# The state-space group norm of three groups, moved to later slots of the weight stream

## The chip, the cores and the metric

The kernel runs on one core of a Trainium2 chip. Its time is the device time of one execution in microseconds (us); a run gives the median of several. TensorE multiplies matrices, VectorE, ScalarE and GpSimd work on vectors, and SyncE issues DMAs. Each engine takes its instructions in order and waits on semaphores that others raise.

## What is computed

The reference is a network of four layers, two of one kind (`first_block`) and two of another (`second_block`), on 256 tokens of width 1024. The change touches only the state-space branch of the first kind, which occurs twice:

```
proj = einsum('bld,de->ble', rms_norm(h, norm1_w[l]), w_in[l])
z, xbc, dt_f, dt_b, sc_b, sc_c, sc_v = split(proj)
y_f, y_b = ssd_chunked(...), flip(ssd_chunked(flip(...)))     # 16 heads of 64, 4 groups of 4 heads, two directions
y = y_f + y_b + xs * d_skip
y = y.reshape(bsz, length, 1024) * silu(z)                      # the gate
yg = y.reshape(bsz, length, 4, 256)                             # four groups of 256 channels
yg = yg * rsqrt(mean(yg * yg, axis=-1) + RMS_EPS)               # the group norm
y_ssd = yg.reshape(bsz, length, 1024) * norm_w
h = h + einsum('ble,ed->bld', concatenate([y_ssd, y_sc]), w_out[l])
```

The other half of the mix, `y_sc`, is a short convolution of three further parts of `proj`.

## The kernel before

All weights are read once. They come in chunks of 128 x 2048 values (1 MB). A chunk is loaded by SyncE into one of three raw buffers. It is then split into a high part (fp32r, `split_hi`, ScalarE, L1231) and a low part (raw minus high, `split_lo`, VectorE, L1671), each in two halves of 128 x 1024, into one of two buffers. TensorE multiplies high weights by high and low inputs, and low weights by high inputs, 48 weight loads and matmuls for a chunk (L542). A split into a buffer waits until the chunk before last is multiplied (`chunk_done`), so ScalarE and VectorE split chunk c + 2 while TensorE multiplies chunk c + 1.

Around this stream the order of everything else is written out by hand, in slots. Slot c is what an engine does between chunk c and the next: on TensorE after the matmuls of chunk c (`slot(c)`), on ScalarE and VectorE around their split of chunk c + 2. There, `late(c)` stands before the split and `extras(c)` behind it. In a layer of the first kind chunks 0 to 8 are xbc and dt, 9 to 12 are z, 13 to 24 are the short convolution's three parts in turn, and 25 to 32 are w_out (25 to 28 for `y_sc`, 29 to 32 for `y_ssd`).

The 16 heads are worked on in pairs p = 0 to 7. In slot 10 + 2p ScalarE makes the first head's decays (`drops(p, 0)`: four operations, L1317), their exp (L1322), and the second head's four (`drops(p, 1)`). Their exp is in `late` of slot 11 + 2p. In that slot VectorE multiplies both by the masked scores (`heads_decayed`, L1863). In slot 12 + 2p TensorE multiplies by the inputs (`heads(p)`, L872). SyncE loads the decay rows for the next pair (L419) once the pair's exps are done.

A group g is two pairs, and its norm goes through six steps:

- `group_gate(g)`, VectorE: adds the skip to the heads' sums (two operations, L1879), multiplies by the gate (L1881).
- `group_squares(g)`, ScalarE: L1326.
- `group_norm(g)`, TensorE: sums of squares by matmuls with ones (L880).
- `group_rsqrt(g)`, VectorE: sums times 1/256 plus eps (`ask_roots`, L1699), a power by GpSimd (L1137), and two diagonal matrices (`root_diagonals`, L1706).
- `group_spread(g)`, TensorE: ones times diagonals, which gives the roots in all partitions (L888).
- `group_scale(g)`, VectorE (L1891), `group_hi(g)`, ScalarE (L1330), and `group_lo(g)`, VectorE (L1898): the scaled output and its two parts, the inputs of w_out.

`GROUP_END` is {14: 0, 18: 1, 22: 2, 26: 3}. Gate and squares of a group are in the slot of its second pair, sums and roots one slot later, spread and the rest two slots later. `group_hi` stands in front of `drops` in ScalarE's extras, and `group_squares` behind them. The gate of a group waits until the low part of the group before is made, since both use the buffer `yb`. Odd groups use another PSUM bank than even ones. VectorE's short-convolution work lies in the same slots: in 14, 17, 20 and 23 a product (L1971) ahead of `late`, and the outer taps (L1846, L1849) behind the split; in 15, 18, 21 and 24 a product (L1981) ahead of `late`, and a low part (L1987) behind the split. ScalarE begins slots 13, 16, 19 and 22 with a copy (L1390) that VectorE waits for.

Of the kernel before, what the change touches and what calls it, by code (L numbers as in the profile page):

```python
# [11 lines left out]
TOK = SEQ // P  # L12
# [4 lines left out]
GROUPS = 4  # L17
# [169 lines left out]
DT_CHUNK = 1  # L187
PAIR_SLOTS = [12, 14, 16, 18, 20, 22, 24, 26]

GROUP_END = {PAIR_SLOTS[2 * g + 1]: g for g in range(GROUPS)}  # L190
ROW_SLOTS = [c - 2 for c in PAIR_SLOTS]
EARLY_TAPS = 3
CONV_OPS = {2: 4, 3: 2, 4: 7, 5: 4, 6: 4, 7: 4, 8: 4, 9: 9, 10: 8, 11: 4, 12: 4, 13: 4, 14: 2, 15: 2, 16: 2, 17: 2, 18: 4, 19: 8, 20: 8,
# [6 lines left out]
def build(nc, a, consts, out):  # L200
# [4 lines left out]
    with ExitStack() as ctx:  # L205
# [66 lines left out]
        sums = sqb[0:32, 2:4, :]  # L272
# [11 lines left out]
        acc = [ctx.enter_context(nc.psum_tensor(f"bank{i}", [P, 512], f32)) for i in range(4)]  # L284
# [39 lines left out]
        y2_ready, gsq_ready, gstat, gdiag, gbc = sem("y2_ready"), sem("gsq_ready"), sem("gstat"), sem("gdiag"), sem("gbc")  # L324
        y3_ready, y_hi, mixssd_ready = sem("y3_ready"), sem("y_hi"), sem("mixssd_ready")
# [199 lines left out]
        def _(pe):  # L525
# [290 lines left out]
            for l in range(DEPTH):  # L816
# [58 lines left out]
                def group_norm(g):  # L875
                    b = acc[2 + g % 2]
                    pe.wait_ge(gsq_ready, l * 4 + g + 1)
                    for m in range(2):
                        for t in range(TOK):
                            last = mm(b[:, t:t + 1], sqb[:, m, t * P:(t + 1) * P], K("ones", 1),  # L880
                                      start=m == 0 and t == 0, stop=m == 1, skip_group_check=True)
                    last.then_inc(gstat, 1)

                def group_spread(g):
                    b = acc[2 + g % 2]
                    pe.wait_ge(gdiag, l * 4 + g + 1)
                    for t in range(TOK):
                        last = mm(b[:, t * P:(t + 1) * P], K("ones"), diag[:, t, :], start=True, stop=True)  # L888
                    last.then_inc(gbc, 1)

                def slot(c):

                    if c in PAIR_SLOTS:
                        heads(PAIR_SLOTS.index(c))
                    if c - 1 in GROUP_END:
                        group_norm(GROUP_END[c - 1])
                    if c - 2 in GROUP_END:
                        group_spread(GROUP_END[c - 2])

                for c in range(1, 25):  # L900
                    if c == DT_CHUNK:
# [4 lines left out]
                    if c == 5:  # L906
                        pe.wait_ge(dta_ready, l + 1)
                        pe.sem_inc(waited, 1)
                        for i in range(2):
                            for t in range(TOK):  # L910
                                k = 2 * i + t
# [37 lines left out]
                for j in range((FF_PAIRS - 1) // 2):  # L949
                    for i in range(2):  # L950
                        c, x = C1_FFN + 2 + 3 * i, cx + j * 6
# [16 lines left out]
            for l in range(DEPTH):  # L968
# [114 lines left out]
                for q in range(2):  # L1083
                    for i in range(2):
                        for t in range(TOK):
                            k = 2 * q + i
# [19 lines left out]
                for j in range((FF2_PAIRS - 1) // 3):  # L1106
                    for i in range(3):
                        c, x = C2_FF + 1 + 2 * i, cx + j * 6
# [3 lines left out]
                        n = l * FF2_PAIRS + j * 3 + (DEPTH * FF_PAIRS + i + 1)  # L1112
# [105 lines left out]
        def _(act):  # L1218
# [64 lines left out]
            for l in range(DEPTH):  # L1283
# [5 lines left out]
                if l == 0:  # L1289
                    act.wait_ge(pt_ready, 2)  # L1290
                    for q in range(DEPTH):
                        for i in range(2):
                            off, n = P1_LATE + 88 * i, 88 + 2 * i
# [30 lines left out]
                def group_squares(g):  # L1324
                    act.wait_ge(y2_ready, l * 4 + g + 1)
                    A(sqb[:, 0:2, :], yb, ACT.Square).then_inc(gsq_ready, 1)  # L1326

                def group_hi(g):
                    act.wait_ge(y3_ready, l * 4 + g + 1)
                    A(hidh[:, 2 * g:2 * g + 2, :], yb, ACT.Copy).then_inc(y_hi, 1)  # L1330
# [5 lines left out]
                def extras(c):  # L1336
                    if c == 5:
                        act.wait_ge(dtT, l + 1)
                        A(dtok[:].rearrange("p a b -> p (a b)"), acc[0][:, 0:128], ACT.Copy).then_inc(dtok_ready, 1)
                    if c == 6:  # L1340
                        act.wait_ge(cs_done, l + 1)
                        A(sums, acc[2][0:32, :].rearrange("p (d t) -> p d t", d=2), ACT.Copy).then_inc(sums_ready, 1)
                        A(diag[:, 2, :], acc[3][:, 0:128], ACT.Copy).then_inc(cs_ready, 1)
                    if c - 2 in GROUP_END:
                        group_hi(GROUP_END[c - 2])
                    if c in ROW_SLOTS:
                        p = ROW_SLOTS.index(c)
                        drops(p, 0)
                        heads_exp(p, 0)
                        drops(p, 1)  # L1350
                    if c in GROUP_END:
                        group_squares(GROUP_END[c])

                for c in range(9):
                    multiplied(c, cx)
# [9 lines left out]
                    for m in range(2):  # L1365
                        k = 2 * q + m
# [8 lines left out]
                for q in range(4):  # L1375
                    c = 9 + q
# [10 lines left out]
                for j in range(4):  # L1387
                    c, u = 13 + 3 * j, 12 + 3 * j
# [8 lines left out]
                    for m in range(2):  # L1397
                        k = 2 * j + m
# [68 lines left out]
                for j in range((FF_PAIRS - 1) // 2):  # L1467
                    for i in range(2):
                        x, xr, y = cx + j * 6, cr + j * 2, ux + j * 4
                        c = C1_FFN + 2 + 3 * i  # L1470
# [25 lines left out]
            for l in range(DEPTH):  # L1496
# [69 lines left out]
                for c in range(28):  # L1566
# [16 lines left out]
                    else:  # L1583
                        k = 2 * (c - 16)
# [16 lines left out]
                for q in range(2):  # L1601
                    act.wait_ge(conv_back, l * 2 + q + 1)
                    for m in range(2):
                        k = 2 * q + m
# [36 lines left out]
                for j in range((FF2_PAIRS - 1) // 3):  # L1641
                    for i in range(3):
                        x, xr, y = cx + j * 6, cr + j * 2, ux + j * 3
                        c = C2_FF + 1 + 2 * i
# [14 lines left out]
        def _(dve):  # L1659
# [37 lines left out]
            def ask_roots(sums, n, scale):  # L1697

                ts(small[:, 16:16 + n], sums, scale, EPS, MUL, ADD).then_inc(spread_var, 1)  # L1699

            def root_diagonals(k, n, signal):

                y = small[:, 24:24 + n]
                dve.wait_ge(spread_root, k + 1)
                for i in range(n):
                    last = ts(diag[:, i, :], ident, y[:, i:i + 1], None, MUL)  # L1706
                last.then_inc(signal, 1)

            def rsqrt_diagonals(k, sums, n, scale, signal):

                ask_roots(sums, n, scale)
                root_diagonals(k, n, signal)

            def root(r, t, centred):

                v, y = norm_small[:, 2, t:t + 1], norm_small[:, 3, t:t + 1]
# [120 lines left out]
            for l in range(DEPTH):  # L1837
# [34 lines left out]
                def group_gate(g):  # L1872

                    if g == 0:
                        dve.wait_ge(pc_ready, l * 2 + 2)
                    dve.wait_ge(y_done, l * 8 + 2 * g + 2)
                    for m in range(2):
                        k = 2 * g + m
                        chain(stt(out=yb[:, m, :], in0=xbc[:, k, :], scalar=p1("d_skip", k), in1=half(acc[2 + g % 2], m), op0=MUL, op1=ADD))  # L1879
                    chain.sync()  # L1880
                    stt(out=yb, in0=yb, scalar=0.5, in1=zz[:, 2 * g:2 * g + 2, :], op0=MUL, op1=MUL).then_inc(y2_ready, 1)  # L1881

                def group_rsqrt(g):
                    dve.wait_ge(gstat, l * 4 + g + 1)
                    rsqrt_diagonals(l * 4 + g, acc[2 + g % 2][:, 0:TOK], TOK, 1.0 / 256, gdiag)

                def group_scale(g):
                    dve.wait_ge(gbc, l * 4 + g + 1)
                    for m in range(2):
                        k = 2 * g + m  # L1890
                        last = stt(out=yb[:, m, :], in0=yb[:, m, :], scalar=p1("ssd_norm", k), in1=acc[2 + g % 2][:, 0:SEQ], op0=MUL, op1=MUL)  # L1891
                        if m == 0:
                            chain(last)
                    last.then_inc(y3_ready, 1)

                def group_lo(g):
                    dve.wait_ge(y_hi, l * 4 + g + 1)
                    tt(hidl[:, 2 * g:2 * g + 2, :], yb, hidh[:, 2 * g:2 * g + 2, :].bitcast(f32), SUB).then_inc(mixssd_ready, 1)  # L1898
# [6 lines left out]
                def extras(c):  # L1905
                    if c in (7, 8):
                        t = c - 7
                        for q in range(2):
                            dve.wait_ge(xT_done, l * 4 + 2 * t + q + 1)
                            b = acc[2 * t + q][:, :].rearrange("p (h d) -> p h d", d=64)  # L1910
                            for d in range(2):
                                col = dtok[:, t, 16 * d + 8 * q:16 * d + 8 * q + 8].unsqueeze(2).to_broadcast([P, 8, 64])
                                tt(xdt[:, d, t, 512 * q:512 * q + 512].rearrange("p (h d) -> p h d", d=64), b, col, MUL).then_inc(xdt_ready, 1)
                    if c in (9, 10):
                        for g in range(2 * (c - 9), 2 * (c - 8)):
                            mask_scores(g)
                    if c - 2 in GROUP_END:
                        group_scale(GROUP_END[c - 2])
                    if c - 2 in GROUP_END:
                        group_lo(GROUP_END[c - 2])  # L1920
                    if c in GROUP_END:
                        if GROUP_END[c]:
                            dve.wait_ge(mixssd_ready, l * 4 + GROUP_END[c])
                        group_gate(GROUP_END[c])
                    if c - 1 in GROUP_END:
                        group_rsqrt(GROUP_END[c - 1])

                for c in range(9):
                    multiplied(c, cx)
# [24 lines left out]
                for q in range(4):  # L1954
                    c = 9 + q
# [7 lines left out]
                for j in range(4):  # L1963
                    c, u = 13 + 3 * j, 12 + 3 * j
# [93 lines left out]
                for j in range((FF_PAIRS - 1) // 2):  # L2058
                    for i in range(2):
                        x, y = cx + j * 6, ux + j * 4  # L2060
                        c = C1_FFN + 2 + 3 * i
# [20 lines left out]
            for l in range(DEPTH):  # L2082
# [114 lines left out]
                for c in range(28):  # L2197
                    kind, b = list2[c][0], ring[c % RING]
                    if kind == "gate":
                        k = 2 * (c - 16)  # L2200
# [256 lines left out]
```

## Time and profile before

| | |
|---|---|
| median of 3 runs | 1683.14 us (1682.93 to 1683.48) |
| the profiled execution | 1682.33 us, span 1680.5 us |
| mean granted TensorE clock | 0.998 |
| busy: TensorE matmul, weight load | 1662.5 us (99%), 1481.4 us (88%) |
| busy: VectorE, ScalarE, GpSimd | 1331.1 us (79%), 980.9 us (58%), 64.4 us (4%) |
| landing of a decay-row load, median | 4.7 us from its issue |

The profile is of one execution. Busy shares are over the whole span. Matmuls are pipelined and their ends are modelled, so TensorE is read best from its weight loads (PEld), whose starts and idle times are recorded. In a timeline a row is a group of like instructions in order of time. The slots 12 to 32 of the first layer lie between about 94 and 226 us, those of the second between about 499 and 631.

### The profile page before, as it was taken

The numbers are of one execution on the slowest core, as the hardware profiler recorded it, in microseconds if no ns is written. First come the engines' busy times: TensorE is split into PE (matmuls) and PEld (weight loads), VectorE is DVE, ScalarE is ACT, GpSimd is POOL, SyncE is SP. The second block draws the span as 40 slices with busy tenths as digits, with TensorE's granted clock in tenths as the row PEclk, the third lists the DMA queues.
The fourth block names the chain that finished last, engine by engine and source line by source line (L and its number), as shares of the span: only waits on it lengthen the run. The fifth ranks groups of instructions, "written<-read, shape, count | busy, mean of one in ns | idle before, by whom it ended". The sixth has DMA issues, their size and how long they took to land.

```text
span 1680.5 us, 27054 instructions
## 1 busy us (share of the span) xinstructions
PE 1662.5 (99%) x10683; PEld 1481.4 (88%) x10690; DVE 1331.1 (79%) x2077; ACT 980.9 (58%) x1631; POOL 64.4 (4%) x79
## 2 busy tenths in 40 slices
PE   9999999999999999999999999999999999999998
PEld 7999888888999988888899889888879988978886
DVE  7877678888877758888899998766679999786666
ACT  5567556565757656666644875545454487555444
POOL 2000000000200000000000011000000000100000
PEclk9999999999999999999999999999999999999999
DMA  7665555555556646555466454656547645466553
GB/s 241 187 190 176 180 172 195 183 199 163 176 176 190 189 161 203 190 197 190 162 203 200 151 188 154 212 188 196 180 148 225 203 150 176 156 208 200 187 190 100
DMA packets 237788, 308.11 MB, mean 183 GB/s; under 512 B 6531, under 2 KB 198749, under 8 KB 237661
## 3 DMA queue, kind: packets, MB, share of 16 engines
q1 hardware_dynamic: 237353, 306.26, 56.7%
q8 instruction: 85, 1.39, 0.4%
q14 instruction: 42, 0.34, 0.1%
q10 hardware_dynamic: 308, 0.12, 0.0%
HBM read 301.04 MB, written 1.11 MB: 180 GB/s over the span
## 4 chain that ended last, share of the span: by engine, by line
PE 88%; DVE 8%; ACT 2%; issue 1%; POOL 0%; POOLq 0%; DVEq 0%; ACTq 0%
PE ring_banks L542 65%; PE bank L542 17%; DVE weights_lo L1671 3%; DVE conv_sums L2110 1%; PE bank L872 1%; PE bank L981 1%; PE bank L992 1%; PE ring_banks L784 1%; ACT weights_hi L1231 1%; PE bank L880 0%; PE bank L832 0%; PE bank L1017 0%; ACT decay L1317 0%; PE bank L797 0%; DVE pair L2241 0%
## 5 line engine op out<-in xcount | busy, mean ns | idle before, releaser
L1671 DVE TENSOR_TENSOR weights_lo<-raw_weights,weights_hi 128x1024 fp32r<-128x1024 f32 (+1 forms) x550 | 643.5, 1211 | 98.4 <-ACT weights_hi L1231 97.2
L542 PE MATMUL ring_banks<-input_parts,weights_hi 128*128 128x256 f32 (+1 forms) x4000 | 691.6, 325 | 5.3 <-DVE weights_lo L1671 2.0
L1231 ACT ACTIVATE weights_hi<-raw_weights 128x1024 fp32r<-128x1024 f32 (+1 forms) x552 | 544.2, 1036 | 194.3 <-PE bank L542 94.9
L542 PEld LDWEIGHTS ring_banks<-input_parts,weights_hi 128*128 128x128 f32 x4000 | 592.8, 190 | 67.8 <-issue 9.9
L542 PE MATMUL ring_banks<-input_parts,weights_lo 128*128 128x256 f32 x2752 | 373.7, 283 | 0.0
L542 PEld LDWEIGHTS ring_banks<-input_parts,weights_lo 128*128 128x128 f32 x2752 | 356.7, 191 | 7.3
L542 PE MATMUL bank<-weights_hi,hidden_hi 128*128 128x512 f32 x432 | 111.3, 392 | 0.0
L542 PE MATMUL bank<-weights_hi,hidden_lo 128*128 128x512 f32 x432 | 110.0, 389 | 0.0
L542 PE MATMUL bank<-weights_lo,hidden_hi 128*128 128x512 f32 x432 | 109.9, 389 | 0.0
L2110 DVE SCALAR_TENSOR_TENSOR conv_sums<-conv_padded,params_second_layer,conv_sums 128x256 f32<-128x256 f32 x240 | 99.2, 480 | 0.0
L542 PEld LDWEIGHTS bank<-weights_hi,hidden_lo 128*128 128x128 f32 x432 | 81.1, 188 | 16.9
L542 PEld LDWEIGHTS bank<-weights_lo,hidden_hi 128*128 128x128 f32 x432 | 81.1, 188 | 16.9
L542 PEld LDWEIGHTS bank<-weights_hi,hidden_hi 128*128 128x128 f32 x432 | 78.0, 189 | 14.1
L1633 ACT ACTIVATE pair<-ring_banks,params_second_layer 128x256 f32<-128x256 f32 x64 | 26.9, 472 | 101.3 <-PE ring_banks L542 101.2
L2339 DVE TENSOR_TENSOR pair<-ring_banks,pair 128x512 f32<-128x512 f32 x32 | 22.1, 691 | 71.9 <-ACT pair L1633 71.9
L542 PE MATMUL ring_banks<-weights_hi,hidden_hi 128*128 128x512 f32 x192 | 75.7, 394 | 0.0
L542 PE MATMUL ring_banks<-weights_hi,hidden_lo 128*128 128x512 f32 x192 | 74.8, 390 | 0.0
L2018 DVE TENSOR_TENSOR pair<-ring_banks,pair 128x512 f32<-128x512 f32 x42 | 29.0, 692 | 40.0 <-ACT pair L1443 31.1
L542 PE MATMUL ring_banks<-weights_lo,hidden_hi 128*128 128x512 f32 x192 | 49.4, 392 | 0.0
L1317 ACT ACTIVATE decay<-squares,diagonals 128x256 f32<-128x256 f32 (+1 forms) x128 | 47.4, 442 | 0.3 <-DMA squares<-decay_rows 0.3
L1863 DVE TENSOR_TENSOR decay<-decay,masked_scores 128x768 f32<-128x768 f32 x32 | 29.7, 955 | 22.2 <-ACT pair L1390 11.4
L542 PE MATMUL ring_banks<-hidden_hi,weights_hi 128*128 128x256 f32 x192 | 47.1, 285 | 0.0
(267 smaller groups left out, 1703.8 us busy)
## 6 DMA issues: line engine op xcount, KB each, us to landing
raw_weights<-in_w_in SPq DMA_DIRECT2D x103, 1024.0 KB, 5.3
raw_weights<-in_w_ff SPq DMA_DIRECT2D x64, 1024.0 KB, 5.5
raw_weights<-in_w_ffn_up SPq DMA_DIRECT2D x44, 1024.0 KB, 5.1
raw_weights<-in_w_ffn_down SPq DMA_DIRECT2D x22, 1024.0 KB, 4.9
raw_weights<-in_w_out SPq DMA_DIRECT2D x16, 1024.0 KB, 5.2
squares<-decay_rows SPq DMA_DIRECT2D x16, 512.0 KB, 4.7
raw_weights<-in_w_o SPq DMA_DIRECT2D x8, 1024.0 KB, 5.1
pair<-pair SPq DMA_DIRECT2D x64, 64.0 KB, 2.9
```

Of the source, the lines that this page charges most:

```text
L542: return mm(o, w, x, start=first, stop=last, skip_group_check=True)
L784: mm(b[:, :], zt[:, 0:P], zt[:, :], start=True, stop=True, skip_group_check=True)
L872: last = mm(o, xdt[:, d, t, h * 64:h * 64 + 64], decay[:, i, e0:e0 + n], start=e0 == 0, stop=e0 == 384)
L981: last = mm(acc[r][:, lo:hi], q, k, start=True, stop=True)
L1231: A(whi[:, t, i * n:(i + 1) * n], raw[:, s, i * n:(i + 1) * n], ACT.Copy).then_inc(hi_done, 1)
L1317: chain(A(decay[:, i, e0:e0 + n], head_rows[:, r0 // SEQ, i, r0 % SEQ:r0 % SEQ + n], ACT.Relu, bias=cs_tok[:, k, e:e + 1], scale=-1.0))
L1633: last = A(tmp[gs % 3][:, m, :], wide_low(u + gx)[:, m, :], ACT.Identity, bias=pc2[:, ds(k, 1)], scale=1.0)
L1671: tt(wlo[:, t, r], raw[:, s, r], whi[:, t, r].bitcast(f32), SUB).then_inc(w_ready, 1)
L1863: tt(decay[:, i, :], decay[:, i, :], scores[:, h // 4, :], MUL).then_inc(v_ready, 1)
L2018: tt(b[:], wide_high(u + side), b[:], ADD).then_inc(ring_free, 1)
L2110: ins = stt(out=cacc[:, k, :], in0=src, scalar=w, in1=cacc[:, k, :], op0=MUL, op1=ADD)
L2339: tt(t[:], wide_high(u + gx), t[:], ADD).then_inc(ring_free, 1)
```

## The change

Four tables, one for each kind of step, take the place of `GROUP_END`. For groups 0 to 2 the gate and the squares move one slot later, the sums and the root's request one later, the diagonals two later (and away from the request), and the spread, the scale, hi and lo two later. Sums and spreads now stand in slots in which TensorE has heads, behind them. For group 3 nothing moves, but scale, hi and lo of group 2 now stand ahead of its gate in slot 26. No instruction is added or removed.

```diff
@@ -187,7 +187,10 @@
 DT_CHUNK = 1
 PAIR_SLOTS = [12, 14, 16, 18, 20, 22, 24, 26]
 
-GROUP_END = {PAIR_SLOTS[2 * g + 1]: g for g in range(GROUPS)}
+GATE_SLOTS = {15: 0, 19: 1, 23: 2, 26: 3}
+SUM_SLOTS = {16: 0, 20: 1, 24: 2, 27: 3}
+DIAGONAL_SLOTS = {17: 0, 21: 1, 25: 2, 27: 3}
+SPREAD_SLOTS = {18: 0, 22: 1, 26: 2, 28: 3}
 ROW_SLOTS = [c - 2 for c in PAIR_SLOTS]
 EARLY_TAPS = 3
 CONV_OPS = {2: 4, 3: 2, 4: 7, 5: 4, 6: 4, 7: 4, 8: 4, 9: 9, 10: 8, 11: 4, 12: 4, 13: 4, 14: 2, 15: 2, 16: 2, 17: 2, 18: 4, 19: 8, 20: 8,
@@ -892,10 +895,10 @@
 
                     if c in PAIR_SLOTS:
                         heads(PAIR_SLOTS.index(c))
-                    if c - 1 in GROUP_END:
-                        group_norm(GROUP_END[c - 1])
-                    if c - 2 in GROUP_END:
-                        group_spread(GROUP_END[c - 2])
+                    if c in SUM_SLOTS:
+                        group_norm(SUM_SLOTS[c])
+                    if c in SPREAD_SLOTS:
+                        group_spread(SPREAD_SLOTS[c])
 
                 for c in range(1, 25):
                     if c == DT_CHUNK:
@@ -1341,15 +1344,15 @@
                         act.wait_ge(cs_done, l + 1)
                         A(sums, acc[2][0:32, :].rearrange("p (d t) -> p d t", d=2), ACT.Copy).then_inc(sums_ready, 1)
                         A(diag[:, 2, :], acc[3][:, 0:128], ACT.Copy).then_inc(cs_ready, 1)
-                    if c - 2 in GROUP_END:
-                        group_hi(GROUP_END[c - 2])
+                    if c in SPREAD_SLOTS:
+                        group_hi(SPREAD_SLOTS[c])
                     if c in ROW_SLOTS:
                         p = ROW_SLOTS.index(c)
                         drops(p, 0)
                         heads_exp(p, 0)
                         drops(p, 1)
-                    if c in GROUP_END:
-                        group_squares(GROUP_END[c])
+                    if c in GATE_SLOTS:
+                        group_squares(GATE_SLOTS[c])
 
                 for c in range(9):
                     multiplied(c, cx)
@@ -1706,11 +1709,6 @@
                     last = ts(diag[:, i, :], ident, y[:, i:i + 1], None, MUL)
                 last.then_inc(signal, 1)
 
-            def rsqrt_diagonals(k, sums, n, scale, signal):
-
-                ask_roots(sums, n, scale)
-                root_diagonals(k, n, signal)
-
             def root(r, t, centred):
 
                 v, y = norm_small[:, 2, t:t + 1], norm_small[:, 3, t:t + 1]
@@ -1880,9 +1878,9 @@
                     chain.sync()
                     stt(out=yb, in0=yb, scalar=0.5, in1=zz[:, 2 * g:2 * g + 2, :], op0=MUL, op1=MUL).then_inc(y2_ready, 1)
 
-                def group_rsqrt(g):
+                def group_root(g):
                     dve.wait_ge(gstat, l * 4 + g + 1)
-                    rsqrt_diagonals(l * 4 + g, acc[2 + g % 2][:, 0:TOK], TOK, 1.0 / 256, gdiag)
+                    ask_roots(acc[2 + g % 2][:, 0:TOK], TOK, 1.0 / 256)
 
                 def group_scale(g):
                     dve.wait_ge(gbc, l * 4 + g + 1)
@@ -1914,16 +1912,17 @@
                     if c in (9, 10):
                         for g in range(2 * (c - 9), 2 * (c - 8)):
                             mask_scores(g)
-                    if c - 2 in GROUP_END:
-                        group_scale(GROUP_END[c - 2])
-                    if c - 2 in GROUP_END:
-                        group_lo(GROUP_END[c - 2])
-                    if c in GROUP_END:
-                        if GROUP_END[c]:
-                            dve.wait_ge(mixssd_ready, l * 4 + GROUP_END[c])
-                        group_gate(GROUP_END[c])
-                    if c - 1 in GROUP_END:
-                        group_rsqrt(GROUP_END[c - 1])
+                    if c in SPREAD_SLOTS:
+                        group_scale(SPREAD_SLOTS[c])
+                        group_lo(SPREAD_SLOTS[c])
+                    if c in GATE_SLOTS:
+                        if GATE_SLOTS[c]:
+                            dve.wait_ge(mixssd_ready, l * 4 + GATE_SLOTS[c])
+                        group_gate(GATE_SLOTS[c])
+                    if c in SUM_SLOTS:
+                        group_root(SUM_SLOTS[c])
+                    if c in DIAGONAL_SLOTS:
+                        root_diagonals(l * 4 + DIAGONAL_SLOTS[c], TOK, gdiag)
 
                 for c in range(9):
                     multiplied(c, cx)
```

## Rows read from the trace of the kernel before

**Rows 1.** The page: the chain of work that ended last, by engine.

```profile
PE 88%; DVE 8%; ACT 2%; issue 1%; POOL 0%; POOLq 0%; DVEq 0%; ACTq 0%
```

**Rows 2.** Waits of TensorE's weight loads: us in total, times, longest us.

```profile
PEld bank L880 <- ACT squares L1326: 1.2, 4, 0.3
```

**Rows 3.** Busy time in one stretch, granted clock, DMA share, GB/s.

```profile
225.00:236.00 11.00, 10.79 (x76) 8.99 (x76) 7.84 (x20) 6.88 (x15) 1.11 (x2) 1.00 0.29 96
```

**Rows 4.** Timeline of TensorE's weight loads, layer 0: start, us, line, [idle before].

```profile
109.24 3.90 PEld L542 LDWEIGHTS ring_banks<-input_parts,weights_hi 128*128 128x128 f32 x32 [0.17 <-issue]
...
143.36 0.97 PEld L880 LDWEIGHTS bank<-constants,squares 128*128 128x128 f32 x8 [0.32 <-ACT squares L1326]
...
165.24 3.90 PEld L542 LDWEIGHTS ring_banks<-input_parts,weights_hi 128*128 128x128 f32 x32 [0.17 <-issue]
...
170.98 0.98 PEld L880 LDWEIGHTS bank<-constants,squares 128*128 128x128 f32 x8
171.89 3.90 PEld L542 LDWEIGHTS ring_banks<-input_parts,weights_hi 128*128 128x128 f32 x32
...
177.84 1.28 PEld L872 LDWEIGHTS bank<-decay,x_times_dt 128*64 128x64 f32 x16
179.29 0.52 PEld L888 LDWEIGHTS bank<-diagonals,constants 128*128 128x128 f32 x4 [0.17 <-DVE diagonals L1706]
179.73 0.19 PEld L542 LDWEIGHTS ring_banks<-weights_hi,hidden_hi 128*128 128x128 f32 x1
...
192.30 0.19 PEld L542 LDWEIGHTS ring_banks<-weights_hi,hidden_hi 128*128 128x128 f32 x1 [0.17 <-issue]
...
197.65 1.08 PEld L880 LDWEIGHTS bank<-constants,squares 128*128 128x128 f32 x8
```

**Rows 5.** Timeline of VectorE in the same stretch.

```profile
115.30 0.69 DVE L1981 TENSOR_TENSOR pair<-pair,ring_banks 128x512 f32<-128x512 f32 x1 [0.67 <-PE ring_banks L542]
116.20 1.83 DVE L1863 TENSOR_TENSOR decay<-decay,masked_scores 128x768 f32<-128x768 f32 x2 [0.21 <-ACT decay L1322]
117.94 2.35 DVE L1671 TENSOR_TENSOR weights_lo<-raw_weights,weights_hi 128x1024 fp32r<-128x1024 f32 x2
120.21 0.69 DVE L1987 TENSOR_TENSOR hidden_lo<-pair,hidden_hi 128x512 fp32r<-128x512 f32 x1
120.81 0.16 DVE L1699 TENSOR_SCALAR small<-bank 128x2 f32<-128x2 f32 x1
...
126.13 0.87 DVE L1891 SCALAR_TENSOR_TENSOR diagonals<-diagonals,params_first_layer,bank 128x256 f32<-128x256 f32 x2
...
141.05 0.87 DVE L1879 SCALAR_TENSOR_TENSOR diagonals<-xbc,params_first_layer,bank 128x256 f32<-128x256 f32 x2
...
144.09 1.83 DVE L1863 TENSOR_TENSOR decay<-decay,masked_scores 128x768 f32<-128x768 f32 x2 [1.44 <-ACT pair L1390]
...
175.91 0.88 DVE L1846 SCALAR_TENSOR_TENSOR pair<-pair,params_first_layer 128x255 f32<-128x255 f32 x2
...
177.62 0.15 DVE L1699 TENSOR_SCALAR small<-bank 128x2 f32<-128x2 f32 x1
178.59 0.48 DVE L1706 TENSOR_SCALAR diagonals<-constants,small 128x128 f32<-128x128 f32 x2 [0.81 <-POOL small L1137]
```

**Rows 6.** Timeline of ScalarE in the same stretch.

```profile
127.03 0.63 ACT L1330 ACTIVATE hidden_hi<-diagonals 128x512 fp32r<-128x512 f32 x1 [2.26 <-DVE diagonals L1891]
127.57 1.48 ACT L1317 ACTIVATE decay<-squares,diagonals 128x256 f32<-128x256 f32 x4
129.08 0.84 ACT L1322 ACTIVATE decay<-decay 128x768 f32<-128x768 f32 x1
129.83 1.48 ACT L1317 ACTIVATE decay<-squares,diagonals 128x256 f32<-128x256 f32 x4
...
143.28 0.60 ACT L1390 ACTIVATE pair<-ring_banks 128x512 f32<-128x512 f32 x1
...
144.51 2.00 ACT L1231 ACTIVATE weights_hi<-raw_weights 128x1024 fp32r<-128x1024 f32 x2
```

## The prediction

> **What bounds the kernel now.** I read the page first. The chain that ended last is 88% TensorE and 8% VectorE [rows 1]: weight chunks follow one another on TensorE without a pause. Next came the waits of the weight-load side of TensorE, where a stall shows most cleanly. In the whole span its waits for the squares of the group norm (L880) come to 1.2 us over 4 waits [rows 2]. So all that the present placing of the norm costs TensorE is those 1.2 us. The granted clock is 1.00 in a stretch where TensorE was idle several tenths [rows 3]. Then I read the three engines' timelines of layer 0, slots 15 to 28; layer 1 repeats them. Each layer has two of the four waits, in slots 15 and 19, of 0.3 us each.
>
> **What TensorE's own order costs.** From weight load to weight load [rows 4]: a w_in chunk takes 5.74 us to a norm (165.24 to 170.98), 5.95 to heads (171.89 to 177.84); heads take 1.45 (177.84 to 179.29, with 0.17 idle), a norm's sums 0.91, a spread 0.44. The chunk before the last norm, of w_out, takes 5.35. The change has three fewer stops per layer between chunks, but the stop itself costs nothing that goes away: chunk to norm has no idle, and the 0.21 and 0.17 around heads stay. Sums behind heads stand nowhere in the trace; heads to spread and heads to chunk are the nearest, and say 0.17 at most either way. I take 0, and keep 6 x 0.17 = 1.0 us both ways for the range. So TensorE's work is unchanged, and all turns on when the squares are ready.
>
> **The chain that ends at the sums.** From the start of the gate on VectorE to the start of the sums is 2.31 us, two passes, one product, the squares on ScalarE (141.05 to 143.36) [rows 4, 5]. I now follow the new order, slot by slot. Before, the gate follows the outer taps in an even slot, which has no decays. The new slots 15, 19 and 23 are the odd ones, where VectorE also does both decay products (116.20 to 117.94, 1.74), and TensorE's only grace is that heads (1.45) come first in the next slot.
>
> *Group 0, gate in slot 15.* Chunk 15 is done at 115.30 as now. VectorE: 0.90 to the decays, 1.74 decays, 2.27 weight split, 0.60 low product [rows 5], gate at 120.8, sums possible at 123.1. TensorE: without the sums in slot 15 chunk 16 starts at 109.24 + 5.74 = 114.98, heads at 120.93, sums' turn at 122.38. Wait 0.7 us; now it is 0.3.
>
> *Group 1, gate in slot 19.* TensorE goes on at 123.1 + 0.91 = 124.0 (chunk 17), 129.8 (18), 135.7 heads, 137.2 spread of group 0, 137.6 (19). Chunk 18 is done at 129.8 + 6.06 = 135.8, where 6.06 is start to release (109.24 to 115.30). VectorE in slots 17 and 18: product when chunk 17 is done (130.1), 0.60, decays 1.74, split 2.27, taps 1.71 (175.91 to 177.62), diagonals 0.48 (178.59), giving 136.4 to 136.9: the diagonals stand 0.2 us before the spread wants them. Then product 0.90, split 2.27, low product 0.60: the scale starts at 140.5. ScalarE has had the hi split done since about 137.8 and sits in front of the hi part of group 0 until scale + 0.90 = 141.4 (126.13 to 127.03 [rows 5, 6]); behind it in its queue stand the decays of pair 4. These take 0.54 + 1.51 + 0.75 + 1.51 = 4.3 us (127.03, 127.57, 129.08, 129.83 [rows 6]). So the copy that opens slot 19 starts at 145.8, though chunk 19 was done at 137.6 + 6.06 = 143.6: ScalarE is 2.1 us late. VectorE waits for that copy: decays at +0.81 (143.28 to 144.09), 146.6; split 148.3; gate 150.6; sums possible at 152.9. TensorE: chunk 20 at 143.3, heads at 149.3, sums' turn at 150.7. Wait 2.1 to 2.2 us; now 0.32. Today the same ScalarE stall falls in slot 16 and is made good by slot 18, whose gate has no decays ahead of it.
>
> *Group 2, gate in slot 23.* Let chunk 23 start at t. VectorE: done t + 6.06, product 0.60, decays 1.74, and 0.6 more because the second exp is late. (In slot 22 ScalarE reaches the hi part of group 1 at t + 2.9 and ends the decays' second exp 0.54 + 1.51 + 0.75 + 1.51 + 0.84 later, at t + 8.1; VectorE would want it at t + 7.5.) Then 0.1 to the split, 2.27 split, 1.71 taps, 2.31: t + 15.4. TensorE: 5.74 + 5.95 + 1.45 = t + 13.1. Wait 2.2 us, of which 1.6 stand even if ScalarE were on time. Now it is 0.
>
> *Group 3, gate still in slot 26*, but scale and low part of group 2 now stand ahead of it. From chunk 26 done: hi split's first half 1.1 (half of the 2.00 of the two at 144.51, and the start), lo split 2.27, scale to hi part 0.90 and hi part to low part 0.67 (126.13, 127.03, 127.70), low part 0.60, gate chain 2.31: 7.8. TensorE: heads 1.45, spread 0.44, chunk 27 5.35, less 0.1: 7.1. Wait 0.7 us; now none (197.65 follows 192.30 by the work alone [rows 4]).
>
> **What goes and gives nothing.** The square-root trip over GpSimd no longer stands between ask and diagonals for three groups, about 0.8 us of VectorE idleness each. After the ask in slots 16 and 20 VectorE has to wait for the next chunk anyway, so this hides. ScalarE's squares leave slots 14, 18 and 22, where the decays of the next pair are made, but the two chains above start from waits, and not from that work. The decay-row loads on SP's queue follow the second exp of each pair, and land about 5 us later (the page's median is 4.7), which is before they are wanted: the exp of slot 19 ends at 147.1, the decays for which the rows are loaded start at 155.5. No DMA and no instruction is added. Heads of group 2 need the scale of group 0 (new: 140.5, wanted 149.3): still ahead. The w_out chunks 31 and 32 need group 3's low part, in slot 28 as before: 5.5 us ahead, as now.
>
> **The sum.** Per layer 0.7 + 2.15 + 2.2 + 0.7 = 5.75 us of waits, less 0.6 to 0.7 of today's: +5.1; two layers +10.2. The same walk over the old order gives waits of 0.3, 0.4, 0.1 and 0 where the rows have 0.3, 0.3, 0, 0, so it errs high by about 0.1 a wait; I take +10. Nothing gives it back: TensorE is the chain before and after the stretch, and the splits run one or two chunks ahead. The profiled execution took 1682.33 us (span 1680.5), 0.8 below the median 1683.14 of the runs. 1682.33 + 10 = 1692.3 profiled, and 1693.0 as a median.
>
> **A rule of the skill.** The rows show clock 1.00 through TensorE waits of a few tenths [rows 3]; none has a wait of 2 us in mid-kernel. The Trainium skill, "TensorE: Matmul & The Clock Gate" (HAM oscillation — how this bites in real kernels), says that too long an idle gap makes the gate fall back to half rate, so that the next burst starts cold. Whether the new waits are long enough for that no row here can tell; it is the third rival.
>
> **Rivals.**
> 1. *The waits vanish (not slower).* Heads in front of the sums give 1.45 us of cover, the spread gets a slot of its own, and no stall is left: two layers lose 2 x 0.6. 1683.1 - 1.2 = 1681.9. For it speaks that ScalarE and VectorE are at 58% and 79%. Against it: the chain of slot 23 holds 1.6 us without any lateness elsewhere. It decides at one point: whether the gate of slots 19 and 23 starts within 2.31 us of the end of the heads, or before. Chance 4%, with "the change moves nothing that TensorE feels".
> 2. *Half of it.* ScalarE isn't late in slot 19, because the scale of slot 18 comes earlier than I have it; then group 1 waits 0.1, and group 2 1.6: 0.7 + 0.1 + 1.6 + 0.7 - 0.6 = 2.5 per layer, 1688.1. For it: all depends on one queue order. Against: the rows of slot 16 now show the same 2.26 us stall of ScalarE in front of a hi part and the same 4.3 us behind it. Chance 8%.
> 3. *The clock falls in the 2 us waits.* The four long ones would each be followed by matmuls at 1.2 GHz. One chunk after each at half rate costs at most its own 5.74 again, so up to 4 x 5.7 on top: 1700 to 1716. Chance 3%.
> 4. *The lateness feeds itself.* ScalarE and VectorE, now waiting for each other across slots, let a weight split come late as well, and TensorE waits for weights too. The split of chunk 21 ends at 150.6 against a chunk start at 153.8: 3 us of room. If that were gone in one slot per layer, 1695 to 1699. Chance 5%.
>
> **How the numbers follow.** The forecast has 80%, its own range 1690.5 to 1695.0 (eight waits at 0.2 each, 1.0 for the sums behind heads, 0.3 of the runs). For the range I go 1 us further towards rival 2: 1689.5 to 1695.0. A change of 0.2%, 3.4 us, is about what can be told from none. Slower by more: the forecast, rivals 3 and 4, nearly all of rival 2: 0.93. Within: rival 1 and some of 2: 0.05. Faster by more has no mechanism: 0.02.
>
> **What would show it.** After: the weight-load side waits for the squares at L880 eight times, about 11 us in all, near 0.7, 2.1, 2.2, 0.7 in each layer, in slots 16, 20, 24 and 27, and the chunks themselves keep their spacing. ScalarE's longest waits for the scale stand in slot 18. VectorE's waits for GpSimd's roots fall from eight to two. TensorE's clock stays at 1.00. If the L880 waits in slots 20 and 24 are below 1 us, the order of ScalarE's queue was read wrongly; if they are as said and the time doesn't follow, TensorE had room that the page doesn't show.

## The result, and the profile after

The changed kernel takes 1698.93 us (median of 4 runs, 1697.42 to 1699.89) against 1683.18 us before (1682.93 to 1683.48). The ratio is 1.0092, with a 95% interval of 1.0079 to 1.0105: slower by 15.75 us. Forecast were 1693.0 and at most 1695.0. The direction and the place are as forecast, and 6 us more are lost than the sum had. The profiled execution took 1698.79 us, its span is 1697.0 us, the mean granted clock 0.994 (before 0.998).

The page after, its chain of work by engine (as [rows 1]) and by line:

```profile
PE 85%; DVE 10%; ACT 2%; issue 2%; DMA 0%; POOL 0%; SPq 0%; DVEq 0%; POOLq 0%; ACTq 0%
PE ring_banks L545 63%; PE bank L545 17%; DVE weights_lo L1674 4%; DVE conv_sums L2109 1%; PE bank L984 1%; ACT decay L1320 1%; PE bank L995 1%; DVE decay L1861 1%; ACT weights_hi L1234 1%; PE bank L883 0%; PE bank L835 0%; DVE diagonals L1877 0%; PE bank L1020 0%; PE bank L875 0%; DVE diagonals L1879 0%
```

TensorE has gone from 88% to 85% of the chain and VectorE from 8% to 10%: more of the time now passes while TensorE waits. The waits of its weight loads for the squares (as [rows 2]; lines after L190 have moved by three, so L880 is L883):

```profile
PEld bank L883 <- ACT squares L1329: 12.7, 8, 2.4
```

Eight waits and 12.7 us, where there were four and 1.2 us. Their places, in the timeline of TensorE's weight loads in layer 0 (as [rows 4]; start, us, line, idle before):

```profile
121.06 1.28 PEld L875 LDWEIGHTS bank<-decay,x_times_dt 128*64 128x64 f32 x16
123.24 0.97 PEld L883 LDWEIGHTS bank<-constants,squares 128*128 128x128 f32 x8 [0.90 <-ACT squares L1329]
...
149.44 1.28 PEld L875 LDWEIGHTS bank<-decay,x_times_dt 128*64 128x64 f32 x16
152.82 0.97 PEld L883 LDWEIGHTS bank<-constants,squares 128*128 128x128 f32 x8 [2.10 <-ACT squares L1329]
153.71 5.40 PEld L545 LDWEIGHTS ring_banks<-input_parts,weights_hi 128*128 128x128 f32 x32
159.04 1.99 PEld L545 LDWEIGHTS ring_banks<-input_parts,weights_lo 128*128 128x128 f32 x16
...
180.53 1.28 PEld L875 LDWEIGHTS bank<-decay,x_times_dt 128*64 128x64 f32 x16
184.23 0.97 PEld L883 LDWEIGHTS bank<-constants,squares 128*128 128x128 f32 x8 [2.43 <-ACT squares L1329]
185.12 0.19 PEld L545 LDWEIGHTS ring_banks<-weights_hi,hidden_hi 128*128 128x128 f32 x1
...
199.75 0.19 PEld L545 LDWEIGHTS ring_banks<-weights_hi,hidden_hi 128*128 128x128 f32 x1
...
206.00 0.97 PEld L883 LDWEIGHTS bank<-constants,squares 128*128 128x128 f32 x8 [0.91 <-ACT squares L1329]
```

The four L883 rows are slots 16, 20, 24 and 27. From heads to sums 1.45 us are work, so the waits proper are 123.24 - 121.06 - 1.45 = 0.73, 152.82 - 149.44 - 1.45 = 1.93, 184.23 - 180.53 - 1.45 = 2.25, and 206.00 - 199.75 - 5.35 = 0.90 us. The forecast had 0.7, 2.15, 2.2 and 0.7. In layer 1 the two long ones are the same to 0.01 us. The new thing is behind the second one: the 32 high weight loads of chunk 21 take 153.71 to 159.04, 5.33 us, where those of chunk 23 take 3.82 in the kernel before. The granted clock, in windows of 1 us each (as in [rows 3]: the window, its length, then busy us and number of instructions of TensorE's matmuls, its weight loads, VectorE, ScalarE and GpSimd; the granted clock is the third number from the end):

```profile
153.00:154.00 1.00, 1.00 (x10) 1.00 (x11) 0.25 (x1) 1.00 (x2) 0.00 (x0) 1.00 1.01 359
154.00:155.00 1.00, 1.00 (x10) 1.00 (x10) 1.00 (x2) 1.00 (x3) 0.00 (x0) 0.91 1.06 371
...
156.00:157.00 1.00, 1.00 (x7) 1.00 (x6) 1.00 (x4) 0.97 (x4) 0.00 (x0) 0.50 0.00 0
...
158.00:159.00 1.00, 1.00 (x9) 1.00 (x9) 0.00 (x0) 1.00 (x4) 0.67 (x1) 0.89 0.85 328
...
187.00:188.00 1.00, 1.00 (x4) 0.71 (x4) 1.00 (x2) 0.98 (x3) 0.00 (x0) 0.50 0.00 0
```

TensorE runs at half clock, 1.2 GHz, for part of chunk 21, after it stood idle for 2.1 us, and again in chunk 25 after 2.4 us. Each time 1.5 to 1.6 us are lost: chunk 21 takes 7.25 us (153.71 to 160.96) against 5.74, and chunk 25 6.98 (185.12 to 192.10) against 5.4. Layer 1 has the same two.

From the first heads (94.6 us) to the end of w_out, layer 0 takes 139.97 us after and 131.86 before, 8.1 more; from there to the same place in layer 1 it is 412.53 against 404.45, again 8.1. Of each, 5.05 are waits (5.81, less 0.76 before: 0.36 and 0.40 by the same reckoning from [rows 4]) and about 3.1 are two stretches of half clock (1.51 and 1.58).

### The profile page after: what moved, and what is told of

It is laid out like the page before. It is cut to its first block, busy times and chain, and to the rows that moved or that the text cites. A ratio compares the mean times of both kernels' runs of the same rounds, so it can differ in the third digit from the quotient of the medians.

```text
span 1697.0 us, 27061 instructions
## 1 busy us (share of the span) xinstructions
PE 1668.8 (98%) x10690; PEld 1486.0 (88%) x10690; DVE 1330.0 (78%) x2077; ACT 982.3 (58%) x1631; POOL 64.5 (4%) x79
## 4 chain that ended last, share of the span: by engine, by line
PE 85%; DVE 10%; ACT 2%; issue 2%; DMA 0%; POOL 0%; SPq 0%; DVEq 0%; POOLq 0%; ACTq 0%
PE ring_banks L545 63%; PE bank L545 17%; DVE weights_lo L1674 4%; DVE conv_sums L2109 1%; PE bank L984 1%; ACT decay L1320 1%; PE bank L995 1%; DVE decay L1861 1%; ACT weights_hi L1234 1%; PE bank L883 0%; PE bank L835 0%; DVE diagonals L1877 0%; PE bank L1020 0%; PE bank L875 0%; DVE diagonals L1879 0%
## 5 line engine op out<-in xcount | busy, mean ns | idle before, releaser
L545 PE MATMUL ring_banks<-hidden_lo,weights_hi 128*128 128x256 f32 x192 | 46.7, 283 | 0.0
```

The source lines that it names most:

```text
L545: return mm(o, w, x, start=first, stop=last, skip_group_check=True)
```

## The experiments

All times are medians. Each kernel is compared with runs of the kernel before on the same chip. Their median was 1683.1 us for the three kernels "the same, and its last long wait filled", "three fillers instead of seven" and "the gate of group 2 alone back", and 1682.8 us for the other four.

### Filling the long waits

`keep_clock(n, bank)` issues n matmuls of 128x512 on zeros into a bank that nobody reads then. The kernel before has it already, for instance eight of them behind the last chunk of the first layer (L784, at 226.49 us), but nowhere in the stretch that was changed.

```diff
 def slot(c):
     ...
+    if c in (20, 24):
+        keep_clock(7, acc[0])
     if c in SUM_SLOTS:
         group_norm(SUM_SLOTS[c])
```

> The changed kernel, with seven 128x512 matmuls on zeros (about 0.2 us each, 1.4 to 1.5 us) between the heads and the group sums in slots 20 and 24, where TensorE waits 2.1 and 2.4 us. They fit into the wait. Theory (10 us of the loss are waits for the squares, 6 us are matmuls at half clock after the two long waits): the clock stays at 1.00, chunks 21 and 25 take 5.7 and 5.4 us again instead of 7.25 and 7.0, and the time is 1683.2 + 10.2 = about 1693. Rival (the clock is no cause, the waits alone do it): the time stays at 1699. Second rival (the filling delays the sums): above 1699.

Measured: 1692.62 us (1692.25 to 1693.23), ratio 1.0059 (1.0046 to 1.0073). TensorE's weight loads around slot 20:

```profile
149.61 1.28 PEld L875 LDWEIGHTS bank<-decay,x_times_dt 128*64 128x64 f32 x16
151.06 1.19 PEld L787 LDWEIGHTS bank<-zeros 128*128 128x128 bf16 x7 [0.17 <-issue]
152.96 0.97 PEld L883 LDWEIGHTS bank<-constants,squares 128*128 128x128 f32 x8 [0.71 <-ACT squares L1331]
153.85 3.89 PEld L545 LDWEIGHTS ring_banks<-input_parts,weights_hi 128*128 128x128 f32 x32
157.67 1.99 PEld L545 LDWEIGHTS ring_banks<-input_parts,weights_lo 128*128 128x128 f32 x16
```

The sums start no earlier than in the changed kernel: 152.96 - 149.61 = 3.35 us behind the heads, against 3.38. But the idle time in front of them is 0.71 us, the record of the granted clock shows no fall until TensorE's work is over, and the 32 loads take 3.82 us again. Added work on zeros, which computes nothing, gives back 6.3 us (5.9 when each time is taken against the kernel before on its own chip: 15.75 and 9.86 over it). So of 16 us, 10 are waits and 6 are the clock.

### Gates back, the rest as changed

```diff
-GATE_SLOTS = {15: 0, 19: 1, 23: 2, 26: 3}
+GATE_SLOTS = {14: 0, 18: 1, 22: 2, 26: 3}
```

> The changed kernel with only the gates and squares of groups 0 to 2 back in slots 14, 18 and 22; sums, diagonals, spreads and scales as changed. Theory (the moved gate makes the long waits): the waits in slots 16, 20 and 24 vanish, the one in slot 27 of 0.7 to 0.9 us stays, the clock stays at 1.00, and the time is 1683.2 + 2 x (0.8 - 0.7) = 1683.2 to 1683.5. Rival (sums and spreads behind heads cost TensorE something by themselves, up to 0.17 us each): 1684 to 1685. Rival (it is the late scale that does it): still above 1690.

Measured: 1682.92 us (1682.11 to 1683.48), ratio 1.0001 (0.9992 to 1.0010). Its waits for the squares:

```profile
PEld bank L883 <- ACT squares L1329: 1.8, 2, 0.9
```

Two are left, those of slot 27 behind scale and low part of group 2. That the time is as before is in part two things that cancel: per layer the waits of slots 15 and 19 are gone (0.76 us), and the later scale brings one of 0.90 us in slot 27. Sums, diagonals and spreads behind heads show no cost of their own (heads to sums take 1.45 us), and all that is lost against the kernel before comes with the gates. TensorE has the same heads and sums here as in the changed kernel, only without the wait between them, and its clock is 1.00 until its work is over; so it is the idle stretch that the falls go with.

### The hi part behind the decays

```diff
-                    if c in SPREAD_SLOTS:
-                        group_hi(SPREAD_SLOTS[c])
                     if c in ROW_SLOTS:
                         ...
                         drops(p, 1)
+                    if c in SPREAD_SLOTS:
+                        group_hi(SPREAD_SLOTS[c])
```

> The changed kernel with one edit in ScalarE's order: in slots 18 and 22 the group's hi part stands behind the decays and their exp and not in front of them. Theory (group 1's wait comes from ScalarE's stall of 3.0 us in slot 18; group 2's would be 1.6 us without any lateness of ScalarE): waits of 0.7, 0.1, 1.6, 0.8 us per layer instead of 0.7, 2.0, 2.3, 0.9, that is 2 x 2.3 = 4.6 to 5 us over the kernel before, and no wait long enough to lower the clock: about 1688. Rival (the waits come from VectorE's load in the odd slots, ScalarE's order is without effect): as the changed kernel, 1699. If the clock still falls after the 1.6 us wait: 1691.

Measured: 1690.13 us (1688.61 to 1691.15), ratio 1.0043 (1.0031 to 1.0056), nearest to the last of the three values expected, 1691. The four rows of sums in layer 0:

```profile
124.03 0.97 PEld L883 LDWEIGHTS bank<-constants,squares 128*128 128x128 f32 x8 [0.90 <-ACT squares L1329]
...
151.71 0.97 PEld L883 LDWEIGHTS bank<-constants,squares 128*128 128x128 f32 x8 [0.21 <-ACT squares L1329]
...
180.88 1.02 PEld L883 LDWEIGHTS bank<-constants,squares 128*128 128x128 f32 x8 [1.70 <-ACT squares L1329]
...
202.62 0.97 PEld L883 LDWEIGHTS bank<-constants,squares 128*128 128x128 f32 x8 [0.91 <-ACT squares L1329]
```

Idle before the sums is 0.90, 0.21, 1.70 and 0.91 us, where the changed kernel has 0.90, 2.10, 2.43 and 0.91. Group 1's wait came from ScalarE's queue, and group 2 keeps 1.53 of its 2.25 us (180.88 - 177.90 - 1.45), the part that VectorE's own queue makes. The stretch shows the clock too: chunk 25, behind the wait of 1.70 us, ran at half clock for a while:

```profile
183.00:184.00 1.00, 1.00 (x4) 0.81 (x3) 1.00 (x2) 1.00 (x4) 0.00 (x0) 0.50 0.00 0
```

### The same, and its last long wait filled

```diff
 (as above, and)
+    if c == 24:
+        keep_clock(5, acc[0])
```

> The kernel with the hi part behind the decays, and five 128x512 matmuls on zeros (about 1.1 us) between heads and sums in slot 24, where its wait of 1.7 us stood and its clock fell once in each layer. Theory (that kernel's 7.4 us over the one before are 4.6 of waits and 2 x 1.5 of half clock): the clock stays at 1.00, and the time is 1690.1 - 3.1 = 1687.0 to 1687.6. Rival (the waits there cost more than the walk says and the clock nothing): 1690.

Measured: 1687.49 us (1686.71 to 1688.48), ratio 1.0026 (1.0016 to 1.0036), with no fall of the clock in the profile before TensorE's work is over. The idle stretch before the sums of slot 24 is 0.76 us instead of 1.70. From end to end of a layer it is 2.3 us over the kernel before, which is what was expected of the waits of this order (4.6 to 5 us over two layers).

### Three fillers instead of seven

```diff
-        keep_clock(7, acc[0])
+        keep_clock(3, acc[0])
```

> The changed kernel with three matmuls on zeros (about 0.6 us) in slots 20 and 24 and not seven, so that TensorE still idles about 1.5 and 1.9 us before the sums. The sums start when they did. Theory A (what lowers the clock is an idle stretch of this size, wherever it falls; a wait of 1.7 us did so twice in another kernel): the clock falls after some or all of the four, 1.5 us each, 1695 to 1699. Theory B (some filling is enough): 1693, as with seven.

Measured: 1696.04 us, with runs from 1692.64 to 1697.44; ratio 1.0074 (1.0061 to 1.0087). The sums of slots 20 and 24 in layer 0, then in layer 1:

```profile
153.33 0.97 PEld L883 LDWEIGHTS bank<-constants,squares 128*128 128x128 f32 x8 [1.59 <-ACT squares L1331]
184.72 0.97 PEld L883 LDWEIGHTS bank<-constants,squares 128*128 128x128 f32 x8 [1.91 <-ACT squares L1331]
564.18 0.97 PEld L883 LDWEIGHTS bank<-constants,squares 128*128 128x128 f32 x8 [1.58 <-ACT squares L1331]
594.06 1.12 PEld L883 LDWEIGHTS bank<-constants,squares 128*128 128x128 f32 x7 [1.91 <-ACT squares L1331]
```

In this run, the slowest of the five, the clock fell behind the first of these waits and, for a stretch twice as long, behind the fourth; behind the second and the third it stayed at 1.00. So the length of the wait alone doesn't decide: 1.59 us brought a fall, and one of 1.91 us didn't. The runs follow their mean granted clock: 1692.64 us at 0.998, as fast as the kernel with seven fillers, 1694.38 at 0.997, 1696.04 and 1696.81 at 0.996, 1697.44 at 0.995. Theory A holds for four of the five runs, with a spread that the kernels without such waits don't have.

### The gate of group 2 alone back

```diff
-GATE_SLOTS = {15: 0, 19: 1, 23: 2, 26: 3}
+GATE_SLOTS = {15: 0, 19: 1, 22: 2, 26: 3}
```

> The changed kernel with the gate and squares of group 2 alone back in slot 22. Theory (each group's wait stands by itself, and each long wait brings one fall of the clock): the wait in slot 24 vanishes with its fall, those of slots 16, 20 and 27 stay: per layer 0.7 + 2.0 + 0.9 - 0.7 = 2.9 of waits and 1.5 of clock, 1682.8 + 8.8 = 1691.6, or 1690 where one of the falls doesn't come. Rival (without the pause in slot 24 the one of group 1 grows or the lateness moves on to other slots): above 1694.

Measured: 1689.48 us (1687.57 to 1691.28), ratio 1.0041 (1.0027 to 1.0054). That is near the lower of the two values of the theory. The wait of slot 24 is gone and the others are unchanged. Two rows of layer 0, then the same two of layer 1, from the same execution:

```profile
152.64 0.97 PEld L883 LDWEIGHTS bank<-constants,squares 128*128 128x128 f32 x8 [2.09 <-ACT squares L1329]
153.53 5.38 PEld L545 LDWEIGHTS ring_banks<-input_parts,weights_hi 128*128 128x128 f32 x32
```

```profile
561.23 0.97 PEld L883 LDWEIGHTS bank<-constants,squares 128*128 128x128 f32 x8 [2.09 <-ACT squares L1329]
562.12 3.89 PEld L545 LDWEIGHTS ring_banks<-input_parts,weights_hi 128*128 128x128 f32 x32
```

The same wait of 2.09 us was followed by a slow chunk in layer 0 (5.31 us to the low loads) and by a fast one in layer 1 (3.82). Layer 0 is 4.2 us longer than before, layer 1 2.7 us: the difference is one fall of 1.5 us. The five runs show it too: 1687.57 us at a mean clock of 0.999, 1689.06 and 1689.48 at 0.998, 1691.07 and 1691.28 at 0.996. An idle stretch of this size may or may not bring the fall; what decides it in a given case stays open.

### A version without waits

```diff
+GATE_SLOTS = {14: 0, 18: 1, 22: 2, 26: 3}
 SUM_SLOTS = {16: 0, 20: 1, 24: 2, 27: 3}
+DIAGONAL_SLOTS = {16: 0, 20: 1, 24: 2, 27: 3}
+SPREAD_SLOTS = {17: 0, 21: 1, 25: 2, 28: 3}
```

> Gates and squares in slots 14, 18, 22 and 26 as in the kernel before, sums and roots behind the heads of slots 16, 20, 24 (27), spread and scale in 17, 21, 25 (28), where ScalarE has no decays to make. Theory: the sums come a heads' length after the squares, no TensorE wait for the norm is left, 0.6 to 0.7 us per layer less than before: 1681.8 to 1682.0. Rival (the stops at a spread of its own, or the diagonals in the same slot as the sums, cost as much): 1683.2 or more.

Measured: 1681.02 us (11 runs, 1680.10 to 1681.74), ratio 0.9990 (0.9981 to 0.9999), the fastest of all kernels here. Slots 16 and 17:

```profile
120.88 1.28 PEld L875 LDWEIGHTS bank<-decay,x_times_dt 128*64 128x64 f32 x16
122.33 0.97 PEld L883 LDWEIGHTS bank<-constants,squares 128*128 128x128 f32 x8 [0.17 <-issue]
123.22 3.89 PEld L545 LDWEIGHTS ring_banks<-input_parts,weights_hi 128*128 128x128 f32 x32
127.03 1.99 PEld L545 LDWEIGHTS ring_banks<-input_parts,weights_lo 128*128 128x128 f32 x16
128.95 0.54 PEld L891 LDWEIGHTS bank<-diagonals,constants 128*128 128x128 f32 x4
129.41 3.90 PEld L545 LDWEIGHTS ring_banks<-input_parts,weights_hi 128*128 128x128 f32 x32
```

The sums follow the heads after 1.45 us, of which the 0.17 idle also stands between heads and a chunk. The stop at the spread costs its own 0.46 us (128.95 to 129.41) and no more. A layer is 0.69 us shorter than before, 1.4 in all, close to the 0.76 us that the two waits of each layer cost. The median is 0.8 us below the range expected. The kernel before is 0.4 us faster on this chip than the 1683.2 from which that was reckoned, and the rest lies within the 1.6 us over which the 11 runs spread; the gain itself is small, and its interval ends just below 1.

## Why the prediction was wrong

**What TensorE's own order costs: right.** Sums behind heads cost nothing that the rows of before didn't show: heads to sums 1.45 and sums to chunk 0.89 us in the version without waits, and 1682.92 us with the gates back.

**The four waits: right.** 5.75 us a layer were forecast, 5.81 measured, less 0.76 of today. Without the clock's share the kernel is 10 us slower (1692.62), which is the forecast's sum. The two longest have the causes given: ScalarE's queue for group 1, VectorE's own load for group 2. The rows after show both. ScalarE in slots 18 and 19:

```profile
137.92 0.62 ACT L1408 ACTIVATE hidden_hi<-pair 128x512 fp32r<-128x512 f32 x1
141.51 0.63 ACT L1333 ACTIVATE hidden_hi<-diagonals 128x512 fp32r<-128x512 f32 x1 [2.97 <-DVE diagonals L1889]
142.05 1.49 ACT L1320 ACTIVATE decay<-squares,diagonals 128x256 f32<-128x256 f32 x4
143.57 0.85 ACT L1325 ACTIVATE decay<-decay 128x768 f32<-128x768 f32 x1
144.32 1.49 ACT L1320 ACTIVATE decay<-squares,diagonals 128x256 f32<-128x256 f32 x4
145.70 0.58 ACT L1393 ACTIVATE pair<-ring_banks 128x512 f32<-128x512 f32 x1
...
152.14 0.63 ACT L1329 ACTIVATE squares<-diagonals 128x512 f32<-128x512 f32 x1 [3.22 <-DVE diagonals L1879]
```

A small slip in the walk didn't matter: its terms give 140.7 for the scale of slot 18, it wrote 140.5, and the trace has 140.6. ScalarE is free at 138.5, stands 2.97 us in front of the hi part (expected 141.4, found 141.51), then makes the decays, and the copy that opens slot 19 starts at 145.70 (expected 145.8), 1.9 us after chunk 19 was done (137.73 + 6.06). VectorE in slots 19, 23 and 26:

```profile
146.50 1.83 DVE L1861 TENSOR_TENSOR decay<-decay,masked_scores 128x768 f32<-128x768 f32 x2 [3.63 <-ACT pair L1393]
148.25 2.35 DVE L1674 TENSOR_TENSOR weights_lo<-raw_weights,weights_hi 128x1024 fp32r<-128x1024 f32 x2
150.52 0.86 DVE L1877 SCALAR_TENSOR_TENSOR diagonals<-xbc,params_first_layer,bank 128x256 f32<-128x256 f32 x2
...
176.99 0.96 DVE L1861 TENSOR_TENSOR decay<-decay,masked_scores 128x768 f32<-128x768 f32 x1 [0.56 <-ACT decay L1325]
177.94 2.36 DVE L1674 TENSOR_TENSOR weights_lo<-raw_weights,weights_hi 128x1024 fp32r<-128x1024 f32 x2
...
181.93 0.86 DVE L1877 SCALAR_TENSOR_TENSOR diagonals<-xbc,params_first_layer,bank 128x256 f32<-128x256 f32 x2
...
201.39 0.87 DVE L1889 SCALAR_TENSOR_TENSOR diagonals<-diagonals,params_first_layer,bank 128x256 f32<-128x256 f32 x2
...
203.69 0.87 DVE L1877 SCALAR_TENSOR_TENSOR diagonals<-xbc,params_first_layer,bank 128x256 f32<-128x256 f32 x2
```

The decays at 146.50 wait for that copy, the split follows at 148.25, the gate at 150.52 (expected 150.6). In slot 23 the second decay product waits for its exp (176.99), and decays, split and taps stand ahead of the gate (181.93). In slot 26 the scale (201.39) stands ahead of the gate of group 3 (203.69), as the prediction had it. That slot 27 waits 0.9 us and not 0.7 is two small terms: from scale to gate it is 2.30 us and not 2.17, and the scale starts 0.06 later than walked.

**The sum: wrong by a missing term.** The step that failed is "TensorE's clock stays at 1.00": the sum puts what the clock does behind the four long waits at nothing, and leaves it to the third rival, "The clock falls in the 2 us waits", at 3%. This is no alternative to the forecast, since it comes on top of the forecast's own waits, and belongs in the sum as a fifth term of every layer, of 3.1 us. The rival's size was off as well. Up to 5.7 us for each of the four long waits were named, as if a whole chunk ran at half rate; measured are 1.5 to 1.6 us each, 6.3 us over four (1698.93 - 1692.62), which is all that the forecast lacked.

For the 3% the prediction gives no reason. It says itself that no row before can tell, and that is a reason for a larger chance and not for a small one. The row that it read, [rows 3], tells even less than it says: TensorE's matmuls are busy 10.79 of 11.00 us there, so the clock of 1.00 stands beside 0.21 us of idle time. The longest idle stretch of the weight-load side from slot 12 of the first layer on is 0.89 us in the kernel before. Nor could the stated range have reached the result: its three terms add up to 2.9 us either way, 1695.9 at most, and all three are of the waits, the order and the runs.

The Trainium skill, "TensorE: Matmul & The Clock Gate" (HAM oscillation — how this bites in real kernels), has the rule that too long an idle gap brings half rate, and that the burst behind it starts cold. The first half is what happened behind nine of twelve long waits here. The second isn't: in the trace the work behind the wait starts at full clock, and the half rate comes 0.5 to 2.4 us later.

**What goes and gives nothing: right.** VectorE's waits for GpSimd's roots fell from eight (6.5 us) to two (1.6 us), as expected, and this gave nothing. Decay-row loads and w_out chunks show in no wait. The other rivals fell: no case with vanished waits or half of them, and no weight split came late; TensorE's waits for the low parts of weights are 1.6 us in the span, as before (1.5).

## What to carry to other kernels

When a step is moved by one slot, follow each engine's queue through the new slot, with start-to-start times from the timeline; here that gave each of four waits within 0.25 us. "Covered by other work" is true only if the queue that makes the input isn't itself behind: a gate one slot later came 2 us too late, since its slot also held two decay products and a ScalarE that had stood in front of a wait. Then ask of each new idle stretch of TensorE what the clock does behind it: a wait of about 2 us cost 3.5 where the clock fell. If a wait can't be avoided, matmuls on zeros inside it can keep the clock, as long as they leave little of it: here seven did and delayed nothing, and three were too few in four runs of five.

## What the runs showed of the hardware

- Idle stretches of TensorE of 1.6 to 2.4 us in the middle of dense work were followed by a stretch at half clock in 9 of 12 cases (four of four in the changed kernel, two of two with the hi part behind the decays, two of four with three fillers, one of two with the gate of group 2 back). No profile shows one behind an idle stretch of at most 1.1 us between chunks.
- It doesn't come every time: one execution has it behind one wait of 2.09 us and not behind the other. Nor does the longer wait bring it more surely: 1.59 us did and 1.91 us didn't in one execution. That also shows in the runs: kernels with such waits spread over 2.5 to 4.8 us (1692.64 to 1697.44), kernels without over 1.0 to 1.8.
- The half clock comes late. TensorE is back at work at 152.82 us, and still has clock 1.00 from 153 to 154; the half rate stands between about 154.8 and 158.2, by the shares of the windows. Over the nine falls the half rate starts 0.5 to 2.4 us after the work does. So the row of the clock has to be looked for behind the wait and not in it.
